# Last projection of a two-block kernel: two output tiles at once, 1 MB weight loads, splits of 2048 columns

## The reference

```python
def swiglu(h, w_in, w_down):
    gu = h @ w_in
    gate, up = jnp.split(gu, 2, axis=-1)
    return (jax.nn.silu(gate) * up) @ w_down
...
        x = x + merged @ w_out[layer]
        x = x + swiglu(rmsnorm(x, norm_ffn_g[layer]), w_ffn_in[layer], w_ffn_down[layer])
    return rmsnorm(x, norm_final_g)
```

## Time and profile before

| | |
|---|---|
| Time, median of 3 | 2592.17 us |
| Span of the profiled execution | 2590.5 us |
| TensorE busy | 2581.2 us, 100% of the span |
| VectorE, ScalarE busy | 1513.4 us, 1308.9 us |
| Mean rate of the DMA queues | 185 GB/s |
| Last projection on TensorE | from 2342.46 to 2582.9 us |
| From the end of the matmuls to the end of the span | 7.6 us |

### The profile page before, as it was taken

One profiled execution on the slowest core, in us unless ns is written; L12 is line 12 of the kernel. 1 busy time (PEld: TensorE's weight loads), 2 busy tenths in 40 slices (PEclk: granted clock), 3 DMA queues, 4 the chain that ended last, 5 costly groups with the idle time before them and its releaser, 6 DMA issues.

```text
span 2590.5 us, 35914 instructions
## 1 busy us (share of the span) xinstructions
PE 2581.2 (100%) x12518; PEld 2151.6 (83%) x12518; DVE 1513.4 (58%) x1866; ACT 1308.9 (51%) x1721; POOL 83.6 (3%) x96
## 2 busy tenths in 40 slices
PE   9999999999999999999999999999999999999998
PEld 8887788888888888888887888888888888888887
DVE  6657556777777754455667565465545454544444
ACT  5455546555555543355645466434544444454443
POOL 2000000101111100000000000000000000000000
PEclk9999999999999999999999999999999999999999
DMA  7745555666666666665655555655566666666664
GB/s 240 220 147 155 171 187 173 193 187 192 187 188 191 186 198 193 193 200 187 186 172 155 167 150 163 194 189 186 178 195 187 188 188 190 187 189 207 195 193 156
DMA packets 301381, 479.63 MB, mean 185 GB/s; under 512 B 15474, under 2 KB 124132, under 8 KB 301024
## 3 DMA queue, kind: packets, MB, share of 16 engines
q1 hardware_dynamic: 299296, 471.66, 59.5%
q0 software_dynamic: 1808, 6.33, 0.8%
q10 hardware_dynamic: 176, 0.27, 0.1%
HBM read 476.10 MB, written 2.10 MB: 185 GB/s over the span
## 4 chain that ended last, share of the span: by engine, by line
PE 99%; DMA 0%; DVE 0%; ACT 0%; ACTq 0%; issue 0%; DVEq 0%
PE acc L593 25%; PE acc L595 25%; PE acc L594 25%; PE acc L894 12%; PE acc L887 6%; PE tp L621 1%; PE tp L684 1%; PE tp L666 1%; PE tp L676 0%; PE tp L1086 0%; PE tp L730 0%; PE tp L1025 0%; PE tp L1013 0%; DMA X<-in_x_dram 0%; PE tp L744 0%; PE acc L1123 0%
## 5 line engine op out<-in xcount | busy, mean ns | idle before, releaser
L1603 DVE TENSOR_TENSOR WL<-WR,WH 128x1024 fp32r<-128x1024 f32 x890 | 1103.0, 1240 | 976.9 <-ACT WH L1141 976.1
L1141 ACT ACTIVATE WH<-WR 128x1024 fp32r<-128x1024 f32 x890 | 942.4, 1059 | 1158.7 <-PE acc L595 984.3
L593 PE MATMUL acc<-WH,A 128*128 128x512 f32 x1328 | 523.6, 394 | 0.3 <-DVE A L1671 0.3
L595 PE MATMUL acc<-WH,A 128*128 128x512 f32 x1328 | 517.5, 390 | 0.0
L594 PE MATMUL acc<-WL,A 128*128 128x512 f32 x1328 | 517.1, 389 | 0.0
L894 PE MATMUL acc<-A,WH 128*128 128x512 f32 x1408 | 336.4, 391 | 0.0
L894 PEld LDWEIGHTS acc<-A,WH 128*128 128x128 f32 x1408 | 258.6, 188 | 50.0
L593 PEld LDWEIGHTS acc<-WH,A 128*128 128x128 f32 x1328 | 249.4, 188 | 53.7 <-issue 4.0
L595 PEld LDWEIGHTS acc<-WH,A 128*128 128x128 f32 x1328 | 249.2, 188 | 52.7
L594 PEld LDWEIGHTS acc<-WL,A 128*128 128x128 f32 x1328 | 249.5, 188 | 50.0
L593 PE MATMUL acc<-WH,BH 128*128 128x512 f32 x688 | 268.2, 390 | 0.0
(11 more groups left out here) (318 smaller groups left out, 1979.5 us busy)
## 6 DMA issues: line engine op xcount, KB each, us to landing
WR<-in_w_in_dram SPq DMA_DIRECT2D x199, 512.0 KB, 3.8
WR<-in_w_ffn_up_dram SPq DMA_DIRECT2D x176, 512.0 KB, 3.6
WR<-in_w_ffn_down_dram SPq DMA_DIRECT2D x176, 512.0 KB, 4.3
WR<-in_w_ffn_in_dram SPq DMA_DIRECT2D x176, 512.0 KB, 3.8
WR<-in_w_out_dram SPq DMA_DIRECT2D x64, 512.0 KB, 3.6
WR<-in_w_in_dram SPq DMA_DIRECT2D x65, 256.0 KB, 3.1
WR<-in_w_ple_gate_dram SPq DMA_DIRECT2D x32, 512.0 KB, 4.2
WR<-in_w_branch_a_dram SPq DMA_DIRECT2D x16, 512.0 KB, 4.4
```

The source lines that it names most:

```text
L593: pe.matmul(o, H[:, kt + k, cols], WH[:, s, k], start=begin, stop=False)
L595: mm = pe.matmul(o, L[:, kt + k, cols], WH[:, s, k], start=False, stop=end)
L1141: act.activation(WH[:, n % RING], WR[:, n % RING], ACT.Copy).then_inc(hi_done, 1)
L1603: dve.tensor_tensor(WL[:, n % RING], WR[:, n % RING], WH[:, n % RING].bitcast(F32), ALU.subtract).then_inc(lo_done, 1)
```

## The change

The last projection of the second block is staged anew; the first block's projection of the same shape stays as it is.

- Two output tiles of 512 columns are multiplied at once ("a half", 1024 columns), for both row tiles, so four PSUM banks hold sums. Half 0 uses `acc[:, 0]` and `tp[:, 2:4]`, half 1 `acc[:, 1]` and `tp[:, 0:2]` (`summands`).
- A load is a "quad": 256 rows x 1024 columns, 1 MB, four blocks of 128x512. There are 22 in each half, 44 in all. The raw data go alternately into `RAW[0]` and `RAW[1]`. The load of a quad waits until VectorE is through with the quad two earlier (`q_lo`).
- ScalarE rounds 2048 columns in one instruction (`roundings`), VectorE makes 2048 columns of remainders in one (`remainders`). Both write into `SPL`, a ring of eleven blocks that hold high and low part side by side. `quads` gives each quad its four blocks and the count of blocks (`emptied`) that TensorE must have used before they may be written. It places a quad at the start of the ring when four blocks do not fit behind the last: worked through, quads lie at blocks 0, 4, 0, 4, ..., and `emptied` of quad n is 4(n - 1): 168 for quad 43, which is all blocks of quads 0 to 41.
- TensorE uses a quad in 24 matmuls (`eight`) and counts `q_used` by 2 after every 12. The last two quads are held back: TensorE waits for the last of them, and then makes the sums of the four banks one after another, 12 matmuls each, in the order columns 1024 to 1535 of row tiles 0 and 1 (`eights_done`), columns 1536 to 2047 of row tiles 0 and 1 (`rows_done`).
- The tiles of half 0 are added to `X` in the second quad of half 1 and their squares are made behind the fourth and sixth. The third tile's add, squares and gain, and then the norm, stand behind the last quad.
- `fw2` now lies on the first blocks of `BH`; its load waits until the sixth quad of half 1 is used.
- Elsewhere seven semaphores are merged into three (as `gate_half` and `gate_v` into `gate_sum`), with the same instructions waiting for the same events.

```diff
+def quads(orders, slots, entries):
+    made, filled, multiplied, at, rounded, summed, split = [], [0] * slots, 0, 0, 0, 0, 0
+    for half, order in enumerate(orders):
+        sevens = [i for i, (_, seven) in enumerate(order) if seven]
+        for i, (j, seven) in enumerate(order):
+            n, places, emptied = len(made), [], []
+            for size in ((3, 4) if seven else (4,)):
+                at = 0 if at + size > slots else at
+                places.append(at)
+                emptied.append(max(filled[at:at + size]))
+                for k in range(size):
+                    filled[at + k] = multiplied + (k + 1 if seven else 2 * (k // 2 + 1))
+                multiplied += size
+                at += size
+            group = sevens if seven else (0, len(order) - 1)
+            made.append(Quad(n, half, j, seven, n % entries, n // entries + 1, places, emptied, rounded, summed, split,
+                             i == group[0], i == group[-1]))
+            rounded, split = rounded + len(places), split + len(places)
+            summed += 3 if seven else 0
+    return made
...
+SLOTS, ENTRIES = 11, 2
+ORDER2 = [(j, False) for j in range(FKT // 2)]
+QUADS2 = quads((ORDER2, ORDER2), SLOTS, ENTRIES)
+PER_HALF = FKT // 2
...
-        fw2 = sb("fw2", [P, D], at=o3)
+        tail = o3 + 8192
+        junk2 = sb("junk2", [P, NT], at=stationary)
+        RAW = [sb("RAW0", [P, 2, 2 * NT], at=tail), sb("RAW1", [P, 2, 2 * NT], at=stationary + 32768)]
+        SUMS = sb("SUMS", [P, 4, NT], at=o3)
+        SPL = sb("SPL", [P, SLOTS, 2, NT], F32R, at=stationary + 32768 + 8192)
+        FW2_KT = 0
+        fw2 = sb("fw2", [P, D], at=base + FW2_KT * T * 4)
...
+        def summands(half):
+            one = [[acc[:, 0, tb, :], tp[:, 2 + tb, :]] for tb in range(TB)]
+            other = [[acc[:, 1, tb, :], tp[:, tb, :]] for tb in range(TB)]
+            sums, products = (other, one) if half else (one, other)
+            return sums, [products[0][0], products[0][1], products[1][0], products[1][1]]
...
-            with sp.Fori(0, D // NT // 2) as n:
-                for half in range(2):
-                    tile(w_down2, n * (2 * NT) + half * NT, FKT, C_DOWN2, half * FKT // 2, n, FKT)
+            for q in QUADS2:
+                if q.n == 0:
+                    sp.wait_ge(hi_done, C_DOWN2 - RING + 1)
+                if q.n == 1:
+                    sp.wait_ge(hi_done, C_DOWN2 - 2)
+                    sp.wait_ge(lo_done, C_DOWN2 - 2)
+                elif q.n >= ENTRIES:
+                    sp.wait_ge(q_lo, QUADS2[q.n - ENTRIES].split + 1)
+                sp.dma_start(RAW[q.entry][:], rows(w_down2, 2 * q.j, slice(q.half * 2 * NT, (q.half + 1) * 2 * NT))
+                             ).then_inc(w_loaded[q.entry], 16)
...
+            pool.wait_ge(q_used, multiplied_by(QUADS2, PER_HALF + 5))
...
-            def last_h(q):
-                turn_h(FF // NT - 1, False)(q)
-                if q == (FKT - 4) // CHUNK_KT - 1:
+            def block(o, high, low, slot, begin, end):
+                pe.matmul(o, high, SPL[:, slot, 0], start=begin, stop=False)
+                pe.matmul(o, high, SPL[:, slot, 1], start=False, stop=False)
+                return pe.matmul(o, low, SPL[:, slot, 0], start=False, stop=end)
+            def raw_block(o, kt, tb, slot, begin, end):
+                cols = slice(tb * P, (tb + 1) * P)
+                return block(o, BH[:, kt, cols], BL[:, kt, cols], slot, begin, end)
+            def eight(q, between=None):
+                sums, _ = summands(q.half)
+                pe.wait_ge(q_lo, q.split + 1)
+                for k in range(2):
+                    for n in range(2):
+                        for tb in range(TB):
+                            mm = raw_block(sums[tb][n], 2 * q.j + k, tb, q.slots[0] + 2 * k + n, q.opens and k == 0,
+                                           q.ends and k == 1)
+                    mm.then_inc(q_used, 2)
+                    if between is not None and k == 0:
+                        between(1)
+            pe.wait_ge(hb_lo, 2 * (FF // NT) - 2)
+            pe.wait_ge(acc_free[0], A_DOWN2[0])
+            for q in QUADS2[:-2]:
+                if q.n == 2:
+                    pe.wait_ge(acc_free[1], A_DOWN2[1])
                     pe.wait_ge(hb_lo, 2 * (FF // NT))
-            pe.wait_ge(hb_lo, 2 * (FF // NT) - 2)
-            tile(BH, BL, FKT, C_DOWN2, 0, 0, A_DOWN2[0], between=last_h)
-            tile(BH, BL, FKT, C_DOWN2, FKT // 2, 1, A_DOWN2[1])
-            tile(BH, BL, FKT, C_DOWN2, FKT, 0, A_DOWN2[0] + 1)
-            pe.wait_ge(acc_free[1], A_DOWN2[1] + 1)
-            j0, resident = 3 * FKT // 2, FKT // 2 - RING
-            for q in range(resident):
-                chunk(BH, BL, CHUNK_KT * q, C_DOWN2, j0 + q, 1, q == 0, False)
-            for tb in range(TB):
-                cols = slice(tb * P, (tb + 1) * P)
-                for q in range(resident, FKT // 2):
-                    n = C_DOWN2 + j0 + q
-                    if tb == 0:
-                        pe.wait_ge(lo_done, n + 1)
-                    for k in range(CHUNK_KT):
-                        kt = CHUNK_KT * q + k
-                        pe.matmul(acc[:, 1, tb, :], BH[:, kt, cols], WH[:, n % RING, k], start=False, stop=False)
-                        pe.matmul(acc[:, 1, tb, :], BH[:, kt, cols], WL[:, n % RING, k], start=False, stop=False)
-                        mm = pe.matmul(acc[:, 1, tb, :], BL[:, kt, cols], WH[:, n % RING, k], start=False,
-                                       stop=(kt == FKT - 1))
-                mm.then_inc(rows_done, 1)
+                eight(q, turn_h(FF // NT - 1, False) if q.n == 0 else None)
+            sums, _ = summands(1)
+            pe.wait_ge(q_lo, QUADS2[-1].split + 1)
+            for tb, n in ((0, 0), (1, 0), (0, 1), (1, 1)):
+                for q in QUADS2[-2:]:
+                    for k in range(2):
+                        mm = raw_block(sums[tb][n], 2 * q.j + k, tb, q.slots[0] + 2 * k + n, False, q.ends and k == 1)
+                mm.then_inc(rows_done if n else eights_done, 1)
...
+            def roundings(q):
+                if q.n == 0:
+                    act.wait_ge(lo_done, C_DOWN2)
+                    act.wait_ge(chunk_used, C_DOWN2 - 2)
+                elif q.n == 1:
+                    act.wait_ge(chunk_used, C_DOWN2)
+                act.wait_ge(*raw_landed(q))
+                if q.emptied[0]:
+                    act.wait_ge(q_used, q.emptied[0])
+                blocks = raw_blocks(q)
+                act.activation(SPL[:, q.slots[0]:q.slots[0] + 4, 0, :], blocks,
+                               ACT.Copy).then_inc(q_hi, 1)
+            it = FF // NT - 1
+            hi(C_UP2 + 16 * it, range(8, 12))
+            silu_of_gate(it)
+            hi(C_UP2 + 16 * it, range(12, 16))
+            roundings(QUADS2[0])
             act.preload_act_table_set("sqrt_and_others")
-            hi(C_DOWN2, range(8, 4 + FKT // 2))
-            for n in range(1, D // NT):
-                hi(C_DOWN2 + n * (FKT // 2), range(4, 8))
-                squares(slices_of(A_DOWN2), N_END2, [n - 1])
-                hi(C_DOWN2 + n * (FKT // 2), range(8, 4 + FKT // 2))
+            roundings(QUADS2[1])
+            turned_h(it)
+            def whole_slices(n):
+                return x_step, 2 * n + 2
+            for q in QUADS2[2:]:
+                roundings(q)
+                step = q.n % PER_HALF
+                if q.half and step in (3, 5):
+                    squares(whole_slices, N_END2, [step // 2 - 1], junk2)
+            squares(whole_slices, N_END2, [2], junk2)
...
+            def remainders(q):
+                raw, s = raw_blocks(q), q.slots[0]
+                dve.wait_ge(q_hi, q.rounded + 1)
+                dve.tensor_tensor(SPL[:, s:s + 4, 1, :], raw, SPL[:, s:s + 4, 0, :].bitcast(F32),
+                                  ALU.subtract).then_inc(q_lo, 1)
...
+            def add_plain(half, n):
+                sums, _ = summands(half)
+                for tb in range(TB):
+                    xs = x_slice(half, tb, n)
+                    dve.tensor_tensor(xs, sums[tb][n], xs, ALU.add).then_inc(x_step, 1)
+            def weight(n):
+                dve.wait_ge(fg_in, 16)
+                dve.wait_ge(squared, 8 * N_END2 + 2 * (n + 1))
+                xs = X[:, :, n * NT:(n + 1) * NT]
+                dve.tensor_tensor(xs, xs, wide(fw2[:, None, n * NT:(n + 1) * NT], [P, TB, NT]),
+                                  ALU.mult).then_inc(weighted, 1)
+            it = FF // NT - 1
+            lo(C_UP2 + 16 * it, range(8, 16))
+            remainders(QUADS2[0])
+            gated_h(it)
+            remainders(QUADS2[1])
+            turned_h(it)
+            for q in QUADS2[2:]:
+                remainders(q)
+                step = q.n % PER_HALF
+                if q.half and step == 1:
+                    dve.wait_ge(q_used, multiplied_by(QUADS2, PER_HALF - 1))
+                    add_plain(0, 0)
```

(66 more changed lines are left out.)

79 lines of the change are left out of this document (43 added, 36 removed).

## The result

| | before | changed |
|---|---|---|
| Time, median of 6 runs | 2592.10 us (2591.74 to 2592.23) | 2600.32 us (2599.87 to 2601.74) |
| Span of the profiled execution | 2590.5 us | 2598.6 us |
| Ratio changed : before | | 1.0032, 95% interval 1.0022 to 1.0043 |

The changed kernel is 8.2 us slower. The forecast was 2598.9 us, range 2597.0 to 2605.0.

A forecast was written before the change was run, and what follows sets the result against it. TensorE, busy throughout the last projection, was taken to bound the kernel. Stop 4.5 + end 2.0 + gain's load 0.2 = 6.7 us on the 2590.5 span gives 2597.2; medians run 1.7 higher, so 2598.9, range 2597.0 to 2605.0.

The forecast's parts named there:

- TensorE alone bounds, nothing to gain in the middle: Last projection: TensorE never stops, so its 1056 matmuls cost nothing more or less.
- The pace's rival: All matmuls: 13 ns above 213 ns each could vanish, 14 us less, giving 2585; chance 4%.
- Splits: 2048-column splits, continued from 512 and 1024 columns: ScalarE 1.89 us, VectorE 2.31 us, hidden in the steady state.
- The stop: Before the last two quads: TensorE stands 4.5 us (4.2 to 4.8), as quad 43 lies where quad 41 lay.
- The end: After the matmuls: VectorE's earlier work delays row tile 1's final add, +2.0 us (1.4 to 2.5).
- The start and the covers: Stage start costs nothing, at most 0.5 us; splits and additional work fit beside a quad's 5.44 us of matmuls.
- Loads: Raw quad loads of 1 MB take 5.9 us, up to 6.3 free; rival that loads bind: 2606.4, chance 11%.
- The gain's load: After half 1's sixth quad: falls beside one or two weight loads, costing 0 to 0.9 us, taken as 0.2.
- The clock: Rival at the stop: clock falls to half, matmuls after it lose 2.4 us, giving 2601.3; chance 27%.
- the forecast's likeliest case: Whole kernel: full clock through the stop, 2598.9 us (2597.8 to 2600.4); chance 50%.
- the comparison of one stop length with one fall seen: At the stop: about 4.3 us without work set against the clock's fall 4.1 us after the program's last matmuls.

The follow-up runs named there:

- the repaired kernel: Changed kernel with ring room for three quads, third tile's gain folded into its scaling, final four groups row tile by row tile: 2592.03 us, ratio 1.0000.
- the ring for three quads: Changed kernel with four more ring blocks, twelve in all, so three quads fit: 2593.89 us, ratio 1.0008 to the kernel before.
- folding the gain: Changed kernel with the third tile's gain applied in its final scaling, its separate gain pass left out: 2599.26 us, ratio 1.0028 to the kernel before.
- one quad held back: Changed kernel with only the last quad held back, quad 42 used like the others: 2596.66 us, ratio 1.0018 to the kernel before.
- the kernel that was kept busy: Changed kernel with 19 additional unused matmuls of 512 columns ahead of the wait for quad 43: 2598.61 us, ratio 1.0026 to the kernel before.
- splits in halves: Changed kernel with each quad split in two 1024-column instructions per engine instead of one of 2048: 2599.57 us, ratio 1.0030 to the kernel before.
- loads issued later: Changed kernel with each load from the fourth on issued only once TensorE has used the quad three earlier: 2601.59 us, ratio 1.0037.
- one wait in the kernel before: Kernel before with one wait for its last chunk ahead of its last 48 matmuls, replacing a wait at each chunk: 2596.15 us, ratio 1.0014.

## Why the prediction was right

- **TensorE alone bounds, nothing to gain in the middle.** Right. Starts stand 0.227 apart but for the stop and the slow stretch behind it, and the repaired kernel equals the one before. The pace's rival is dead.
- **Splits.** 1.89 and 2.31 us worked out, 1.917 and 2.292 measured; continuing the line from 512 and 1024 columns was good to 2%.
- **The stop.** 4.5 predicted, 4.54 measured, cause shown by the ring for three quads. It could be read from `quads` alone, worked through: with eleven blocks and four in a row needed, only eight are ever used.
- **The end.** +2.0 predicted, 1.96 measured; halved by folding the gain, 4.7 with one quad held back, gone with the fold and rows first together.
- **The start and the covers.** No stop at either, as predicted.
- **Loads.** 5.9 us was mis-sized; 4.9 measured. The term did not enter the sum. From 0.5 to 1 MB the load gained 0.5 us, not the 1.4 that I continued from 256 to 512 KB; the rows of the weights read at once are twice as long. The gain's load cost nothing in place of 0.2: the two weight loads beside it took 4.8 and 5.9 us, within the 6.3 that are free. The prediction had put the 6.6 of the earlier trace rows beside the gain's load; in that trace the loads beside it took 6.4 at most, and the one of 6.6 was issued after 2500 us, far from it.
- **The clock.** Here the forecast's likeliest case lost to the rival. It put 50% on full clock through the stop and 27% on the fall; the fall came in all three profiles with this stop, and, by the times of the kernel that was kept busy, most likely in every execution. The price given was 2.4 us; the profile of the changed kernel has 1.65, two others with the same stop 2.7 and 3.0, and keeping TensorE busy won 1.7. Less the 0.2 us of the gain's load that did not come, that is the difference between 2598.9 and 2600.3. The measured time lies even within the bounds given to the likeliest case (2597.8 to 2600.4), but by another sum, and that is luck. The step that failed is the comparison of one stop length with one fall seen: the delay from the last matmul to the fall is no constant, 4.3 us in the changed kernel's stop and 2.1 in that with the splits in halves, so one fall at 4.1 us said nothing for a stop with 4.4 us without work.

## What to carry to other kernels

Work a ring's placement through with its real counts before trusting the number in its name: blocks that must be contiguous can leave it a quarter smaller (eight of eleven here), and the loss shows only where a wait for the newest entry stands ahead of work on an older one. When tiles are merged to make two at once, the last pair's follow-up work comes due at the end of the kernel, and its order there decided 2 us here where the merged stage itself was worth nothing. Row tile by row tile, with the gain folded into a later step, nothing was late. For a stage whose bounding engine never waits, bigger loads and longer instructions on the other engines are worth nothing; look for what their coarser grain adds at both ends.

## What the runs showed of the hardware

- TensorE's granted clock fell, counted from the end of the last matmul, 2.1 us (splits in halves), 3.2 (loads issued later), 3.8 (gain folded) and 4.3 us (changed kernel) into the stop. Behind the last matmul of the program it fell after 2.1 us with the ring for three quads and after 5.2 with one quad held back. In the profiled execution with one wait in the kernel before, 2.46 us without a matmul brought no fall.
- The slow stretch behind a stop lasted 8 to 15 matmul starts at 0.427 us each. The stop of 4.54 us cost 1.65, 2.7 and 3.0 us on top in three profiles, the one of 3.76 us cost 2.6. The shorter stop was hardly cheaper in time: 2599.57 against 2600.32. Nineteen matmuls without use inside the stop kept the clock full and won 1.7 us.
- A load of 1 MB in rows of 4 KB lands in 4.9 us, one of 0.5 MB in rows of 2 KB from the same matrix in 4.4 (medians; single loads of 1 MB took up to 6.6).
- Issuing the last store 0.5 us sooner did not let the last one land sooner: 2590.0 in both traces.
